# First attention of a two-block transformer kernel: projection tiles placed in every step, scores issued two steps ahead

## What is computed

```python
proj = xn @ w_in[l]
qd, kd, vd, qc, kc, vc, gd, gc = jnp.split(proj, IN_SPLITS, axis=-1)
o_d = diff_attention(qd, kd, vd, ...)
o_c = chunk_attention(qc, kc, vc, chunk_rel_bias[l])
g_d = jax.nn.sigmoid(gd + b_gate[l, :D])
g_c = jax.nn.sigmoid(gc + b_gate[l, D:])
merged = g_d * (o_d @ w_branch_diff[l]) + g_c * (o_c @ w_branch_chunk[l])
h = h + merged @ w_out[l]
h = h + peer(rmsnorm(h, norm2_w[l]), ...)
```

## Time and profile before

| | us |
|---|---|
| median of three timed runs | 1626.13 (1621.11 to 1631.65) |
| the profiled execution | 1634.91 |
| its span | 1633.3 |
| TensorE busy in the span (matmuls) | 1526.4 |
| VectorE busy | 1124.6 |
| ScalarE busy | 728.3 |
| first attention, first scores to transposes of `y` | 120.76 to 233.01 |
| a weight chunk, from issue to landing (median) | 4.9 |

### The profile page before, as it was taken

The page is one execution under the profiler, slowest core; times in us unless marked ns, Lnnn a source line. Parts: engine busy times, 40 slices in busy tenths (PEclk is TensorE's granted clock), DMA queues, the critical chain, the costliest instruction groups (busy, mean ns, idle before and its releaser), DMA issues.

```text
span 1633.3 us, 27671 instructions
## 1 busy us (share of the span) xinstructions
PE 1526.4 (93%) x10710; PEld 1397.5 (86%) x10710; DVE 1124.6 (69%) x1590; ACT 728.3 (45%) x835; POOL 265.1 (16%) x306
## 2 busy tenths in 40 slices
PE   7997889899999999999999999998999897689997
PEld 6986779799999999998888888778997795589976
DVE  5545457589999989846667677667774575677743
ACT  4345563444545454534444444444443357244431
POOL 1201000000010101125454464520000000000000
PEclk9999889899999999999999999999999996789999
DMA  6651225457666577887787787864555440245541
GB/s 238 218 192 68 76 78 184 147 173 250 212 247 228 189 266 268 286 300 276 280 285 288 276 290 282 282 245 152 189 201 177 159 168 26 92 146 202 204 170 62
DMA packets 56290, 329.65 MB, mean 202 GB/s; under 512 B 7472, under 2 KB 7520, under 8 KB 24720
## 3 DMA queue, kind: packets, MB, share of 16 engines
q1 hardware_dynamic: 35856, 259.01, 45.0%
q0 software_dynamic: 20352, 69.47, 12.3%
HBM read 294.90 MB, written 33.55 MB: 201 GB/s over the span
## 4 chain that ended last, share of the span: by engine, by line
PE 55%; DMA 18%; DVE 16%; ACT 9%; issue 2%; SPq 0%; DVEq 0%; ACTq 0%; POOLq 0%
DMA raw<-in_wstream 17%; PE ub L1514 13%; PE ub L1515 13%; PE ub L1516 13%; DVE wl L866 10%; ACT wh L528 6%; PE acc L1514 3%; PE acc L1516 3%; PE acc L1515 3%; PE acc L1700 3%; PE ub L1602 1%; PE acc L1578 1%; PE acc L1478 0%; DVE esel L1210 0%; ACT p_sb L631 0%
## 5 line engine op out<-in xcount | busy, mean ns | idle before, releaser
L866 DVE TENSOR_TENSOR wl<-raw,wh 128x2048 fp32r<-128x2048 f32 x245 | 590.3, 2410 | 332.2 <-ACT wh L528 330.7
L528 ACT CAST wh<-raw 128x2048 fp32r<-128x2048 f32 x245 | 467.7, 1910 | 418.3 <-DMA raw<-in_wstream 318.4
L1514 PE MATMUL ub<-xh,wh 128*128 128x256 f32 x2216 | 627.6, 283 | 14.3 <-DVE gate L968 5.9
L1515 PE MATMUL ub<-xl,wh 128*128 128x256 f32 x2216 | 621.2, 280 | 0.0
L1516 PE MATMUL ub<-xh,wl 128*128 128x256 f32 x2216 | 620.8, 280 | 0.0
L1514 PEld LDWEIGHTS ub<-xh,wh 128*128 128x128 f32 x2216 | 424.0, 191 | 17.3 <-DVE wl L866 15.2
L1515 PEld LDWEIGHTS ub<-xl,wh 128*128 128x128 f32 x2216 | 424.0, 191 | 0.1
L1516 PEld LDWEIGHTS ub<-xh,wl 128*128 128x128 f32 x2216 | 424.0, 191 | 0.0
L1514 PE MATMUL acc<-wh,ah 128*128 128x512 f32 x512 | 200.7, 392 | 2.8 <-DVE al L1257 2.1
L1516 PE MATMUL acc<-wh,al 128*128 128x512 f32 x512 | 199.3, 389 | 0.0
L1515 PE MATMUL acc<-wl,ah 128*128 128x512 f32 x512 | 199.3, 389 | 0.0
(11 more groups left out here) (315 smaller groups left out, 1624.0 us busy)
## 6 DMA issues: line engine op xcount, KB each, us to landing
raw<-in_wstream SPq DMA_DIRECT2D x245, 1024.0 KB, 4.9
gates<-gst POOLq DMA_DIRECT2D x16, 1024.0 KB, 14.7
gl_in<-gates POOLq DMA_DIRECT2D x64, 256.0 KB, 5.1
hidden<-hid POOLq DMA_DIRECT2D x60, 256.0 KB, 4.5
hid<-hidden POOLq DMA_DIRECT2D x60, 256.0 KB, 5.0
resid<-in_x SPq DMA_DIRECT2D x2, 512.0 KB, 4.0
rb<-in_rel POOLq DMA_DIRECT2D x1, 1024.0 KB, 8.2
wb<-in_ffn_post_g POOLq DMA_DIRECT2D x2, 512.0 KB, 3.8
```

Source lines behind the costliest of these rows:

```text
L528: act.copy(wh[:, slot, :], raw[:, slot % RAW, :]).then_inc(w_high, 1)
L866: v.tensor_tensor(wl[:, slot, :], raw[:, slot % RAW, :], wh[:, slot, :].bitcast(F32), ALU.subtract).then_inc(w_low, 1)
L1514: pe.matmul(dst, sh, mh, start=first, stop=False)
L1515: pe.matmul(dst, sh, ml, start=False, stop=False)
```

## The change

The stream of chunks is reordered: the first eight `qk` chunks keep their place as `qkd` (queries and keys of the differential heads), and the last four, `qkc` (those of the chunked heads, wanted from step 16 on), come behind `vc`, ahead of `gate`. In the first attention each of the 24 steps now has one tile (four `qkc` chunks and eight `gate` chunks, two tiles each). The tiles alternate between both banks of `ub`, and all outputs go to `mb[:, 1]`, so that output(n) on TensorE waits until ScalarE has read output(n - 1).

TensorE: scores(0), scores(1), tile 0, then step n is turn(n), scores(n + 2), tile n + 1, output(n). ScalarE: the split for `qkc`'s first chunk, exps(0), exps(1), then step n is output(n - 1), turn(n), exps(n + 2), and in odd steps a split, in even steps from 10 on a gate bias. VectorE: first_bias(0), first_bias(1), first_weights(0), a low part, then step n is first_bias(n + 2), first_weights(n + 1) and, in odd steps, a low part and a `scaled`. The second block's attention (`early` is false there) keeps its order, and the loops over `qk` chunks are written out instead of looped.

```diff
-_sizes = [("qk", 12), ("vd", 4), ("vc", 2), ("gate", 8), ...
+_sizes = [("qkd", 8), ("vd", 4), ("vc", 2), ("qkc", 4), ("gate", 8), ...
@@ ScalarE, attention
+                if early:
+                    exps(0)
+                    exps(1)
+                    for n in range(count):
+                        if n >= 1:
+                            output(n - 1)
+                        turn(n)
+                        if n + 2 < count:
+                            exps(n + 2)
+                        beside(n)
+                    output(count - 1)
+                    return
@@ ScalarE, beside a step
-                if n % 3 == 0 and n:
-                    gate_bias(n // 3 - 1)
-                if n % 3 == 2:
-                    ahead(CH["gate"] + n // 3)
+                if n % 2 == 1 and n < 22:
+                    ahead(CH["qkc"] + (n + 1) // 2)
+                if n % 2 == 0 and n >= 10:
+                    gate_bias((n - 10) // 2)
...
+            ahead(CH["qkc"])
             attention(24, 0, ...)
@@ VectorE
             first_bias(0)
+            first_bias(1)
+            first_weights(0)
+            ahead(CH["qkc"])
             for n in range(24):
+                if n + 2 < 24:
+                    first_bias(n + 2)
                 if n + 1 < 24:
-                    first_bias(n + 1)
-                first_weights(n)
-                if n % 3 == 2:
-                    g = n // 3
-                    ahead(CH["gate"] + g)
-                    v.wait_ge(c_done, CH["gate"] + g + 1)
-                    scaled(gate[:, 2 * g:2 * g + 2, :], 0).then_inc(u_free, 1)
+                    first_weights(n + 1)
+                if n % 2 == 1:
+                    c = (n - 1) // 2
+                    if c < 11:
+                        ahead(CH["qkc"] + c + 1)
+                    v.wait_ge(c_done, CH["qkc"] + c + 1)
+                    dst = qkT[:, 16 + 2 * c:18 + 2 * c, :] if c < 4 else gate[:, 2 * c - 8:2 * c - 6, :]
+                    scaled(dst, (UN["qkc"] + c) % 2).then_inc(u_free, 1)
                 heads_norm(n)
@@ TensorE, attention
                     pe.wait_ge(at_v, n0 + n + 1)
-                    if n >= 2:
-                        pe.wait_ge(at_d, n0 + n - 1)
+                    if n >= (1 if early else 2):
+                        pe.wait_ge(at_d, n0 + n if early else n0 + n - 1)
+                    bank = mb if early else (mb, ub)[b]
...
                 scores(0)
+                if early:
+                    scores(1)
+                    beside(0)
+                    for n in range(count):
+                        turn(n)
+                        if n + 2 < count:
+                            scores(n + 2)
+                        if n + 1 < count:
+                            beside(n + 1)
+                        output(n)
+                    return
@@ TensorE, beside a step
-                g, t = n // 3, n % 3
-                if t < 2:
-                    c, u = CH["gate"] + g, UN["gate"] + g
-                    if t == 0:
-                        pe.wait_ge(w_low, c + 1)
-                        pe.wait_ge(u_free, u + 2)
-                    last = unit_tile(c % RING, 0, t)
-                    if t == 1:
-                        last.then_inc(c_done, 1)
+                c, u = CH["qkc"] + n // 2, UN["qkc"] + n // 2
+                if n % 2 == 0:
+                    pe.wait_ge(w_low, c + 1)
+                    pe.wait_ge(u_free, u + 1)
+                last = unit_tile(c % RING, u % 2, n % 2)
+                if n % 2 == 1:
+                    last.then_inc(c_done, 1)
```

More of the change, by code:

```diff
@@ L45 @@
 AHEAD = RING - 1
-_sizes = [("qk", 12), ("vd", 4), ("vc", 2), ("gate", 8), ("bd", 4), ("bc", 2), ("out", 4),
+_sizes = [("qkd", 8), ("vd", 4), ("vc", 2), ("qkc", 4), ("gate", 8), ("bd", 4), ("bc", 2), ("out", 4),
           ("wq", 4), ("pu", 64), ("pv", 64), ("gu1", 22), ("dn1", 11), ("in2", 7), ("wo", 4),
@@ L55 @@
 TOPK_U = 32
-_usizes = [("qk", 12), ("gate", 8), ("bd", 4), ("bc", 4), ("wq", 4), ("gu1", 22),
+_usizes = [("qkd", 8), ("qkc", 4), ("gate", 8), ("bd", 4), ("bc", 4), ("wq", 4), ("gu1", 22),
            ("in2", 7), ("gu2", 22)]
@@ L601, in _ @@
             act.wait_ge(col_in, 16)
-            normed(0, UN["qk"])
+            normed(0, UN["qkd"])
             split(0, 0)
@@ L607, in _ @@
             split(2, 2)
-            for j in range(4):
+            for j in range(8):
                 ahead(j)
-            with act.Fori(1, 3) as i:
-                for j in range(4):
-                    ahead_at(i * 4 + j, j)
             for c in range(CH["vd"], CH["vd"] + 4):
@@ L623, in _, with attention @@
             act.activation(lams[:, 2:4], lams[:, 0:2], ACT.Exp).then_inc(lam_e, 1)
-            def attention(count, n0, sb_, pb_, pt_, mx_, r_, rr_, blocks_of, out_of, sink=False, beside=None):
+            def attention(count, n0, sb_, pb_, pt_, mx_, r_, rr_, blocks_of, out_of, sink=False, beside=None,
+                          early=False):
                 def exps(n):
@@ L652, in output @@
                     w = P // parts
+                    bank = mb if early else (mb, ub)[n % 2]
                     for r in range(parts):
-                        last = act.activation(dst[:, r * w:r * w + w], (mb, ub)[n % 2][:, 1, r * w:r * w + w],
+                        last = act.activation(dst[:, r * w:r * w + w], bank[:, 1, r * w:r * w + w],
                                               ACT.Copy, scale=rr_[:, n % 4, r:r + 1])
                     last.then_inc(at_d, 1)
+                if early:
[10 more added lines that the diff above has]
+                    return
                 for n in range(count):
@@ L1022, in _ @@
             v.engine_nop().then_inc(lam_s, 2)
[L1023 to L1026, removed]
+            for j in range(4):
+                project(1, j)
+            for c in range(CH["vd"], CH["qkc"]):
                 ahead(c)
@@ L1553, in acc_chunk @@
                 ins.then_inc(c_done, 1)
-            turn_normed(resid, UN["qk"], [(x_in[tt], 16) for tt in range(TT)])
-            for j in range(4):
+            turn_normed(resid, UN["qkd"], [(x_in[tt], 16) for tt in range(TT)])
+            for j in range(8):
                 unit_chunk(j, j, j, j, fresh=j == 0)
@@ L1560, in _ @@
                     scale_row()
-            with pe.Fori(1, 3) as i:
-                for j in range(4):
-                    unit_chunk(i * 4 + j, j, i * 4 + j, j)
             for k in range(4):
@@ L1569, in attention @@
             def attention(count, n0, q_of, k_of, pb_, pt_, v_of, single_of, first=None, beside=None):
+                early = beside is not None
                 def scores(n):
@@ L1601, in output @@
                         for kb in range(1 + b):
-                            last = pe.matmul((mb, ub)[b][:, 1, r * w:r * w + w], pt_[:, b, r * (1 + b) + kb, :],
+                            last = pe.matmul(bank[:, 1, r * w:r * w + w], pt_[:, b, r * (1 + b) + kb, :],
                                              v_of(n, kb, r, w), start=kb == 0, stop=kb == b)
@@ L1613, in attention @@
                         output(n - 1)
-                    if beside is not None:
-                        beside(n)
                     turn(n)
@@ L1823, in layout @@
     parts = {
-        "qk": chunks(tiles(np.concatenate([qd, kd, qc, kc], axis=1))),
+        "qkd": chunks(tiles(np.concatenate([qd, kd], axis=1))),
+        "qkc": chunks(tiles(np.concatenate([qc, kc], axis=1))),
         "vd": wide(vd), "vc": wide(vc), "gate": chunks(tiles(gates)),
```

2 lines of the change are left out of this document (1 added, 1 removed).

## The result

The changed kernel takes 1605.43 us (median of four runs, 1603.76 to 1608.61), the kernel before 1624.17 (four runs, 1621.11 to 1631.65). The ratio is 0.9878 with a 95% interval of 0.9845 to 0.9912: 18.7 us less at the medians, 14 to 25 by the interval. I had forecast 1607 (1596 to 1621) and gave 0.59 to "faster by over 1%". The median is 1.2% lower; the interval just reaches down to 0.9%. One execution of the kernel before, timed beside the experiments further down, took 7219.46 us and is left out of their ratios.

A forecast was written before the change was run, and what follows sets the result against it. It took handovers between engines to bound the attention, in the new order a 9.2 us loop per round. Saving 22.1 us in front and losing 2.9 in the attention gave 1626.1 - 19.2 = 1607 us, range 1596 to 1621.

The forecast's parts named there:

- Front: Projection ahead of the first attention: four chunks leave at 5.53 us each, saving 22.1 us.
- The round: Even plus odd attention step, differential heads: a loop through VectorE, ScalarE and TensorE sets 9.2 us a round.
- The sign in the trace that I named: Attention's odd steps: VectorE waits about 2 us for the high part; TensorE's only wait precedes the odd transposes.
- The chunk half: Attention's chunked heads: the loop is 8.7 us, TensorE's work 8.9, so TensorE decides.
- Start and tail: Attention's ends: step 3's scores done at 9.7 us, step 23's at 102.6, the stage ends at 115.2.
- The head norm inside the loop at step 19: VectorE, attention step 19: eight squares of the head norm lengthen the 8.7 us loop by 1.75.
- The clock: TensorE in the attention: stays at 2.4 GHz despite one wait a round, perhaps one fall near steps 20 to 23.
- the cold-tile rival: Attention: one tile of each round at 1.2 GHz, 1.4 us more a round, 1621 us in total; chance 0.10.
- The rival of 1594 to 1599: Attention: TensorE sets the pace at 7.9 to 8.4 us a round, gain 27 to 32 us; chance 0.14.
- The total: Whole kernel: 22.1 us saved in front less 2.9 us lost in the attention, net 19.2 us.

The follow-up runs named there:

- the second execution of before: The kernel before, unchanged, profiled once more: 1620.27 us (one run), first scores at 117.52, attention 112.8.
- The doubled copy: Changed kernel with each of the attention's twelve scaling copies made twice on VectorE: 1613.69 us, 0.9889 of the kernel before.
- both executions: The changed kernel's first profile, 1604.93 us, and the same kernel unchanged, profiled once more, 1601.49 us (one run).
- the mended split: Changed kernel with ScalarE's splits moved to even steps and VectorE's low parts to the next odd step: 1586.54 us, 0.9744 of the kernel before.
- the best kernel with two: Changed kernel, scores two steps ahead, with all splits in even steps, the first chunk's too: 1588.47 us, 0.9737 of the kernel before.

## Why the prediction was right

**Front.** Forecast 22.1, measured 22.7 against the second execution of before (26.0 against the first). Four times the pace of TensorE was the right count. That I read the pace from the right pair of copies had luck in it: the four distances ahead of it are 7.30, 2.80, 6.57 and 4.50 (60.69, 67.99, 70.79, 77.36, 81.86). Two tiles of 2.72, 5.44 a chunk, say the same as 5.53 without that choice.

**The round.** Forecast 9.2, measured 9.17 in the differential heads, and every link within 0.1 of its term: scores to bias 0.86 for 0.70 and 0.15, bias 0.81 for 0.78 and a handover, cast 1.92 for 1.90, weights 0.99 for 0.94 and a handover. The sign in the trace that I named, VectorE waiting about 2 us for the high part, is there with 2.07, and TensorE's wait of 0.8 to 1.3 ahead of the odd transposes with 1.04. The doubled copy confirms that this is a loop and not a coincidence of numbers.

**The chunk half.** Forecast 8.9 by TensorE; the next copies are 9.06, 8.71 and 8.84 apart (165.64, 174.70, 183.41, 192.25). That TensorE decides there can be read from the trace: from the scores of step 17 on it is busy without a gap, until it waits 1.51 us ahead of step 21's transposes.

```profile
168.00:193.80 25.80, 25.80 (x215) 23.46 (x214) 14.78 (x56) 16.46 (x45) 0.00 (x0) 1.00 0.33 119
```

**Start and tail.** The sum had the attention 115.2, measured 114.2 and 115.6. Step 3's scores were to be done 9.7 after the first ones; VectorE takes them up at 104.65, 9.9 after, of which 0.15 is the handover. Step 23's scores were to be done at 102.6:

```profile
195.89 0.70 PE L1594 MATMUL acc<-qkT 64*128 64x256 f32 x4
```

They end at 196.6, 101.8 after the first, and the tail is 12.4 instead of 12.6. The head norm inside the loop at step 19 cost what I had put down for it: its squares stand between the copy at 192.25 and the even bias,

```profile
192.85 0.28 DVE L1084 CUSTOM_DVE_ANT_0 junk<-y 128x128 f32<-128x128 f32 x1
...
194.66 0.29 DVE L1050 CUSTOM_DVE_ANT_0 s_sb<-acc,rb 128x128 f32<-128x128 f32 x1
```

1.81 us for 1.75. The scores of steps 21 and 23 are 10.54 apart (185.35, 195.89); I had 8.7 + 1.75 = 10.45. (The terms of the tail add up to 112.7 and not to 112.8; it changes nothing.)

**The clock.** I took it to stay at 2.4 GHz through a wait of about 1 us per round, with perhaps one fall near steps 20 to 23. It does in both executions, 1.00 on 100 to 190. The one fall is at 196 to 200 (0.60) in the first, behind the wait of 1.51, and in the tail (0.50) in the second, whose wait at step 21 was 1.40. The Trainium skill's warning (TensorE: Matmul & The Clock Gate, "HAM oscillation — how this bites in real kernels"), that a loop which pauses between bursts can be cold again in every round, did not come true at a pause of 1.04 us per 9.17; with 1.76 per 9.90 it did, behind three waits of five. The case that this section of the Trainium skill describes waits some 3 to 5 us for DMA in each round; no run here has such a loop. Since 0.7 us more of waiting was enough for some falls, the cold-tile rival deserved its 0.10.

**TensorE's pace.** The rival of 1594 to 1599 priced what is to be had without the loop at 8 to 13 us. It is 13.8 in the attention, but that the numbers meet is luck. I multiplied by ten rounds, though in my own sum TensorE set the pace in two of them already. The seven rounds of the differential heads give 8.8 at the 7.91 of the mended split; the rest is 1.7 in the round with the head norm and 3.1 in the tail, which I had not priced. What I did not see is that this rival is one placement away, and that the order of before, with a tile in every step, has it already in the differential heads. I weighed the change as a whole; had I counted the loop for each of its two edits apart, the split behind the odd exponentials would have stood out as a cost of the new order alone.

**The total.** 19.2 us were forecast; 18.7 came at the medians, 22.7 - 1.4 = 21.3 by front and attention against the second execution of before. The stages bear the forecast out; that the totals meet within 2 us is luck as well, as executions of the kernel before alone lie 10 us apart (1621.11 to 1631.65).

**What stays open.** Beyond front and attention, the experiments' medians lie some 5 to 8 us further under before than their profiles' two parts explain (for the moved chunks alone 21.4 + 10.9 = 32 against 40). The part behind the attention varied from 1388.3 to 1400.3 over ten executions of kernels with the same instructions there, and the one execution of before with 1388.4 was also faster than all but one of those timed beside it. Whether late loads behind the attention depend on what precedes them was not tried.

## What to carry to other kernels

Where several engines with a fixed order hand work round in a circle, add up the links of the circle; if the sum exceeds the busiest engine's work, move the work that needs no answer (here the split of a chunk wanted three units later) to a place that the circle doesn't pass, before adding depth. Software pipelining pays only for latency that nothing else covers: with a dense tile in every step TensorE was full in the differential heads with one step of lookahead, and the best kernel with two has an attention only 2 us shorter (99.7 against 101.9). Time the parts of a combined change apart, since 40 and 21 us made 19 together.

## What the hardware showed that I had not expected

A pause of 1.04 us in a round of 9.17 left the granted clock at 1.00 in every round of the differential heads; of five pauses of 1.76 or 1.77 us in rounds of 9.90 three were followed by a fall and two were not. One of 2.89 us at the tail was followed by 0.50, 1.38 us at the same place was not; 1.51 us at step 21 was followed by 0.60, 1.40 in the second execution was not. So the length of the last pause alone does not tell. And one more operation of 0.73 us, on an engine busy for 63% of the stage, cost 0.73 in each round where it stood in the loop that set the pace. At the same place in VectorE's order it cost nothing once the split of the weights was moved out of that loop.
